# Feed-forward of a decoder layer: remainders at its start moved to VectorE, twelve loads in flight and results finished in place in its second product

## The chip, the cores and the metric

The kernel runs one layer of a decoder on one core of a Trainium2 chip. The metric is the device time of one execution in microseconds; the median of several runs is compared. The clock of the matrix engine (TensorE, "PE" in the profile) has two levels here, 2.4 GHz (granted clock 1.00) and 1.2 GHz (0.50).

## The reference, cut to what matters

The layer has two sub-layers. The change touches only the second, the feed-forward, and its tail:

```python
h = rms_norm(x, g_pre_ffn[l]) * (1.0 + scale_f) + shift_f       # x: (1, 1024, 1024) float32
gu = h @ w_ffn_in[l]                                             # 1024 x 5632
g_part, u_part = gu[..., :D_FF], gu[..., D_FF:]                  # D_FF = 2816 = 22 * 128
y = (jax.nn.silu(g_part) * u_part) @ w_ffn_out[l]                # 2816 x 1024
x = x + gate_f * rms_norm(y, g_post_ffn[l])
```

## The kernel before, in words

All products are float32. Each operand is split into a rounded part `hi` and a remainder `lo = value - hi`; `product` issues three matmuls for every product of blocks (hi*hi, hi*lo, lo*hi). ScalarE ("ACT") makes the `hi`, GpSimd ("POOL") or VectorE ("DVE") the `lo`, SyncE ("SP") issues the DMAs. Every engine runs its own instructions in the order written; semaphores tie them. There is no scheduler: the order in the code is the order on the engine.

**First product** (`h @ w_ffn_in`). Of the 22 column tiles of gate and up, two are computed plainly (`up`, four weight units `N_FF` to `N_FF+3`), 20 (`NW`) by a Winograd-like scheme of seven products of half-size blocks (`wino`, 84 matmuls a tile). It needs four sums of blocks of the activations, T1 to T4 (`t_part` on VectorE, 16 pieces), their `hi` (`t_hi_part`, ScalarE) and their `lo` (`t_lo_part`, GpSimd, L883); for each tile four weight sums (`s_part`, VectorE, L1719), seven `hi` (`ws_hi_part`, ScalarE, L1188) and seven `lo` (`ws_lo_part`, GpSimd, L888); and `ff_pair` (VectorE, L1747 to L1764) puts the seven results together, with two SiLUs on ScalarE. The remainders of the last two plain units are `split_plain` on GpSimd (L894). The stretch in which the plain tiles run, while T1 to T4 and the operands of the first Winograd tile are made, is called the turn.

**Sums for the second product.** `w_ffn_out` takes part in the same kind of scheme with eleven (`KF`) row pairs. For each of them `load_w2` brings 1 MB into `w2t`, GpSimd makes four differences (`add_w2`, L923) in `w2s`, and `store_w2` writes 1 MB to `w2sum_dram`. There is one `w2t` and one `w2s`, so set j+1 cannot be loaded before set j's sums are made, nor summed before set j is stored. GpSimd makes set 0 between the remainders of Winograd tiles 0 and 1, sets 1 to 9 inside its loop, set 10 after the loop. Before the last tile's results ScalarE waits for all 44 sums (`act.wait_ge(w2_sum, 4 * KF)`), and SP stores set 10 before it issues the first loads of the second product, since these use the same memory.

**Second product** (`... @ w_ffn_out`). 77 steps (`DN`): seven products P1, P5, P6, P3, P7, P2, P4 of eleven steps each, twelve matmuls a step (`down`). For step m `load_down` (L717) loads two or three tiles of 256 KB, `add_down` (VectorE, L1810) makes the left sum two steps ahead, `down_hi` (ScalarE, L1257, L1259) and `remainders` (VectorE, L1728, L1731) split both operands into one of eight slots (`RING`). A load may be issued when the load eight places earlier has been consumed. P1 has two loads a step, kept in `a_keep` and `b_keep`; P5 three (A21, A22, T1). `evac_down` adds finished products from PSUM.

**Tail.** For each of eight row tiles: multiply both halves with the column factor `grow` into `fin` (L1854, L1855; for tiles 4 to 7 the right half in `c22`, L1846), reciprocal root of the mean square (squares on ScalarE in `z_square`, L1276; L1857 to L1862), `fin * rstd + x1r` (L1865), and `store_tile`. `fin` has two slots, so from tile 2 on the multiplication waits until an earlier tile has been written out. PSUM of tiles 4 to 7 is complete one tile after another at the end of the last five steps.

Of the kernel before, what the change touches and what calls it, by code (L numbers as in the profile page):

```python
# [25 lines left out]
P = 128  # L26
# [13 lines left out]
def hybrid_layer(nc, x, c, positions, w_ada, b_ada, g_pre_mix, g_post_mix, w_in, b_f, sinks,  # L40
# [166 lines left out]
    RING = 8  # L207
# [8 lines left out]
    dn_raw = [at(f"dn_raw{r}", H0 + (32 * (r // 4) + 4 * (r % 4)) * KB, [P, NT]) for r in range(RING)]  # L216
# [7 lines left out]
    fin = at("fin", R0 + 80 * KB, [P, 2, D])  # L224
# [180 lines left out]

    def dn_src(m, what):
# [3 lines left out]
        return dn_raw[raw_no[m, what] % RING][:, :]  # L410

# [20 lines left out]
    for m in sorted(evacs):  # L432
        p, tt = evacs[m]
        if p >= 2:
            n_ev += {3: 2, 4: 2}.get(p, 1)
            ev_no[p, tt] = n_ev
    SQUARES = [(t, 1) for t in range(NTOK)] + [(t, 0) for t in range(NTOK)]
# [7 lines left out]
    with ExitStack() as ctx:  # L445
# [9 lines left out]
        tile_in = [sem(f"tile_in{k}") for k in range(KD)]  # L455
# [22 lines left out]
        dve_step, pool_step, act_step = sem("dve_step"), sem("pool_step"), sem("act_step")  # L478
# [7 lines left out]
        gcol_ok, diag_ok, grow_ready, grow_ok = sem("gcol_ok"), sem("diag_ok"), sem("grow_ready"), sem("grow_ok")  # L486
# [16 lines left out]
        done = [sem("done0"), sem("done1")]  # L503
# [16 lines left out]
        def _(sp):  # L520
# [159 lines left out]
            with sp.Fori(0, NW // 2 - 1) as it:  # L680
                store_w2(it)
                load_w2(it + 1)
                for par in range(2):
                    sp.wait_ge(fs_lo, it * (2 * NPR) + NPR * (par + 1))
                    load_raw(par, it * (2 * P) + (PLAIN + 2 + par) * P)
                    store_ff(it * 2 + (1 + par), 1 - par, it * 4 + (8 + 2 * par))

            def store_tile(t):
                for hb in range(2):
                    cols = slice(hb * NT, (hb + 1) * NT)  # L690
                    sp.wait_ge(fin_ok, 2 * t + hb + 1)
                    sp.dma_start(out_v[t][:, cols], fin[:, t % 2, cols]).then_inc(done[t % 2], 16)
# [9 lines left out]
            def load_down(m, what, ahead):  # L702
                name, j = dn_step_of(m)
                q = load_no[m, what]
                if q >= RING:
                    sp.wait_ge(*consumed(*ahead[q - RING]))
                row, col = int(what[1]) - 1, int(what[-1]) - 1
                if what[0] == "T":
                    sp.wait_ge(w2_out, 16 * (j + 1))
# [7 lines left out]
                sp.dma_start(dn_src(m, what), src).then_inc(tile_in[q % RING], 16)  # L717
# [7 lines left out]
            for m, what in order_of_loads[:RING]:  # L725
# [4 lines left out]
            sp.wait_ge(w2_out, 16 * KF)  # L730
            for m, what in order_of_loads[RING:]:
# [11 lines left out]
            for i in range(2):  # L743
                sp.wait_ge(done[i], 2 * 16 * (NTOK // 2))

        @block.gpsimd
        def _(pool):
# [132 lines left out]
            def t_lo_part(q):  # L880
                name, k = T_ORDER[q]
                pool.wait_ge(t_hi, q + 1)
                pool.tensor_tensor(t_hl[name][1][:, k], t_fp32(name, k)[:, :], t_hl[name][0][:, k].bitcast(F32), ALU.subtract)\  # L883
                    .then_inc(t_lo, 1)

# [5 lines left out]
            def split_plain(j):  # L891
                n = N_FF + 2 + j
                pool.wait_ge(w_hi_ok, n + 1)
                pool.tensor_tensor(w_hl[1][:, n % 2], wraw[:, n % 2], w_hl[0][:, n % 2].bitcast(F32), ALU.subtract)\  # L894
                    .then_inc(w_split, 1)

            for q in range(2):
                t_lo_part(q)
            split_plain(0)
            for q in range(2, 6):  # L900
                t_lo_part(q)
            split_plain(1)
            for q in range(6, 12):
                t_lo_part(q)
            for i in range(4):
                ws_lo_part(0, 0, i)
            for q in range(12, 16):
                t_lo_part(q)
            for i in range(4, NPR):
                ws_lo_part(0, 0, i)  # L910

            def add_w2(it, what, first):
                n = W2_SUMS.index(what)
# [3 lines left out]
                if what == "T1":  # L917
                    pool.wait_ge(w2t_in, it * 32 + 32)
                    if not first:
                        pool.wait_ge(w2_out, it * 16)  # L920
# [4 lines left out]
            pool.wait_ge(ff_ready, 8)  # L925
            for what in W2_SUMS:
                add_w2(0, what, True)
# [8 lines left out]
            for what in W2_SUMS:  # L936
                add_w2(KF - 1, what, False)

        @block.scalar
        def _(act):  # L940
# [303 lines left out]
            def loaded(m, what):  # L1244
                q = load_no[m, what]
                act.wait_ge(tile_in[q % RING], 32 + 16 * (q // RING + 1))
# [32 lines left out]
            for m in range(3, DN):  # L1279
# [5 lines left out]
                if DN - KF <= m < DN - KF + NTOK:  # L1285
                    z_square(m - DN + KF)
            for t in range(NTOK):
                z_square(NTOK + t)
                act.wait_ge(z_var, t + 1)
# [3 lines left out]
        def _(dve):  # L1293
# [9 lines left out]
            nc.vector.memset(credit[:, 1:2], 0.0).then_inc(ff_ok, 4)  # L1303

# [397 lines left out]

            def mult_plain(ff, ch):
# [17 lines left out]
            def loaded(m, what):  # L1721
                q = load_no[m, what]
                dve.wait_ge(tile_in[q % RING], 32 + 16 * (q // RING + 1))
# [42 lines left out]
            for q in range(8):  # L1766
                t_part(q)
            mult_plain(0, 0)
            for q in range(8, 12):
                t_part(q)  # L1770
            for k in range(KH, KD):
# [4 lines left out]
            for q in range(12, 16):  # L1776
                t_part(q)
            mult_plain(1, 0)
            mult_plain(1, 1)
# [574 lines left out]
```

## Time and profile before

| | us |
|---|---|
| median of 3 runs | 1503.3 (1502.32 to 1504.65) |
| profiled execution, its own time | 1501.47 |
| its span on the core | 1499.7 |
| TensorE busy | 1413.5 (94%) |
| VectorE, ScalarE, GpSimd busy | 977.8, 550.6, 614.3 |
| mean granted clock of TensorE | 0.988 |

Positions are microseconds from the start of the span. The first product with its turn reaches from about 816 to 1261, the second product from 1261 to 1484.5, the tail from there to the end. A matmul of 128x512 is shown with 0.39 us, but they are pipelined: two neighbours start 0.227 us apart at full clock. In a row of the timeline the bracket gives the idle time of the engine ahead of the instruction and what ended it.

### The profile page before, as it was taken

How to read it: one execution, taken by the hardware profiler on the slowest of the kernel's cores; microseconds unless marked ns; L12 is line 12 of the kernel's file. 1: busy time of each engine (PE TensorE's matmuls, PEld its weight loads, DVE VectorE, ACT ScalarE, POOL GpSimd, SP SyncE). 2: the span in 40 equal slices, each digit the busy share in tenths (PEclk: the TensorE clock that was granted, in tenths of full speed). 3: DMA queues.
4: the chain of work that ended last, by engine and by line, in shares of the span. 5: the costliest groups of instructions: out<-in, count | busy, mean ns of one | idle time of the engine just before them, and what ended most of it. 6: DMA issues, size and time to landing. Idle time of an engine off the chain costs nothing. (4 is left out here: it accounts for less than half of the span.)

```text
span 1499.7 us, 19843 instructions
## 1 busy us (share of the span) xinstructions
PE 1413.5 (94%) x6923; PEld 1153.7 (77%) x6923; DVE 977.8 (65%) x1410; ACT 550.6 (37%) x1122; POOL 614.3 (41%) x500
## 2 busy tenths in 40 slices
PE   4899898999999999999999899999999999899995
PEld 2898676777768888888878677888888887678884
DVE  4776867555554766666665877766666664578677
ACT  3711367554552000112243433333333333454452
POOL 0315735242345544334211888766666662000000
PEclk9999999999999999999999999999999999999998
DMA  9401111121222645432332136444444434656754
GB/s 349 130 15 29 48 39 40 53 63 43 92 57 92 165 130 145 121 113 85 99 113 99 52 106 193 140 140 140 140 140 140 140 112 161 225 180 213 245 169 168
DMA packets 174635, 184.63 MB, mean 123 GB/s; under 512 B 15872, under 2 KB 128600, under 8 KB 174048
## 3 DMA queue, kind: packets, MB, share of 16 engines
q1 hardware_dynamic: 168336, 178.87, 38.2%
q10 hardware_dynamic: 6224, 4.77, 1.0%
q8 instruction: 45, 0.74, 0.2%
q14 instruction: 30, 0.25, 0.1%
HBM read 147.94 MB, written 35.68 MB: 122 GB/s over the span
## 5 line engine op out<-in xcount | busy, mean ns | idle before, releaser
L1474 DVE TENSOR_TENSOR pt_lo<-PS,pt_hi 128x512 fp32r<-128x512 f32 (+3 forms) x128 | 74.5, 582 | 97.5 <-ACT pt_hi L1045 97.1
L888 POOL TENSOR_TENSOR ws_lo<-s_tmp,ws_hi 128x512 fp32r<-128x512 f32 x80 | 114.0, 1429 | 58.6 <-ACT ws_hi L1188 58.6
L1874 PE MATMUL PS<-db_hi,da_hi 128*128 128x512 f32 x308 | 121.7, 395 | 8.6 <-DVE db_lo L1731 8.5
L1874 PE MATMUL PS<-T_hi,ws_hi 128*128 128x512 f32 x320 | 124.6, 389 | 1.0 <-POOL ws_lo L888 1.0
L1874 PE MATMUL PS<-T_hi,ws_lo 128*128 128x512 f32 x320 | 124.5, 389 | 0.0
L1874 PE MATMUL PS<-T_lo,ws_hi 128*128 128x512 f32 x320 | 124.5, 389 | 0.0
L1874 PE MATMUL PS<-db_hi,da_lo 128*128 128x512 f32 x308 | 121.3, 394 | 0.0
L1874 PE MATMUL PS<-db_lo,da_hi 128*128 128x512 f32 x308 | 121.1, 393 | 0.0
L1874 PE MATMUL PS<-act_hi,w_hi 128*128 128x512 f32 x288 | 113.8, 395 | 3.1 <-POOL w_lo L894 3.1
L794 POOL CAST w_hi<-wraw 128x1024 fp32r<-128x1024 f32 x39 | 43.0, 1102 | 174.3 <-PE PS L1874 113.0
L1874 PE MATMUL PS<-act_lo,w_hi 128*128 128x512 f32 x288 | 112.7, 391 | 0.0
L1874 PE MATMUL PS<-act_hi,w_lo 128*128 128x512 f32 x288 | 112.6, 391 | 0.0
L1045 ACT ACTIVATE pt_hi<-PS 128x512 fp32r<-128x512 f32 (+3 forms) x128 | 65.2, 510 | 119.7 <-PE PS L2080 101.5
L2001 PE MATMUL PS<-act_hi,w_hi 128*128 128x512 f32 x240 | 95.7, 399 | 5.6 <-DVE nm L1455 5.1
L796 POOL TENSOR_TENSOR w_lo<-wraw,w_hi 128x1024 fp32r<-128x1024 f32 x39 | 99.6, 2553 | 3.2
L1874 PE MATMUL PS<-act_hi,ws_hi 128*128 128x512 f32 x240 | 94.3, 393 | 5.0 <-POOL ws_lo L888 5.0
L836 POOL TENSOR_SCALAR s_row<-s_row,rden 128x128 f32<-128x128 f32 (+7 forms) x64 | 47.1, 749 | 123.9 <-DVE rden L1469 123.8
L2001 PE MATMUL PS<-act_hi,w_lo 128*128 128x512 f32 x240 | 96.1, 400 | 0.0
L2001 PE MATMUL PS<-act_lo,w_hi 128*128 128x512 f32 x240 | 94.4, 393 | 0.0
L1874 PE MATMUL PS<-act_hi,ws_lo 128*128 128x512 f32 x240 | 94.1, 392 | 0.0
L1874 PE MATMUL PS<-act_lo,ws_hi 128*128 128x512 f32 x240 | 93.9, 391 | 0.0
L1106 ACT ACTIVATE sg<-PS 128x512 f32<-128x512 f32 x28 | 16.8, 599 | 207.6 <-PE PS L1874 207.6
(310 smaller groups left out, 3743.1 us busy)
## 6 DMA issues: line engine op xcount, KB each, us to landing
dn_raw<-ff_dram SPq DMA_DIRECT2D x66, 256.0 KB, 3.7
adaraw<-in_w_ada_dram SPq DMA_DIRECT2D x32, 512.0 KB, 4.1
wraw<-in_w_in_dram SPq DMA_DIRECT2D x25, 512.0 KB
wraw<-in_w_ffn_in_dram SPq DMA_DIRECT2D x24, 512.0 KB, 5.1
ff_dram<-sl SPq DMA_DIRECT2D x22, 512.0 KB, 6.6
w2t<-in_w_ffn_out_dram SPq DMA_DIRECT2D x22, 512.0 KB, 6.8
w2sum_dram<-w2s SPq DMA_DIRECT2D x11, 1024.0 KB, 5.8
dn_raw<-w2sum_dram SPq DMA_DIRECT2D x44, 256.0 KB, 3.9
```

The lines of the kernel that those rows point to most:

```text
L794: pool.tensor_copy(w_hl[0][:, slot], wraw[:, slot]).then_inc(w_hi_ok, 1)
L796: pool.tensor_tensor(w_hl[1][:, slot], wraw[:, slot], w_hl[0][:, slot].bitcast(F32), ALU.subtract)\
L836: ins = pool.tensor_scalar(pr, pr, rden[:, r % 4, hd:hd + 1], 1.0, ALU.mult, ALU.mult)
L888: pool.tensor_tensor(ws_hl[i][1][:, :, :], left(par, i), ws_hl[i][0][:, :, :].bitcast(F32), ALU.subtract)\
L1045: nc.scalar.activation(pt_hl[gp % 3][0][:, 0:n], PS[:, 4 + gp % 2, 0:n], ACT.Copy).then_inc(grp_hi, 1)
L1106: nc.scalar.activation(sg[:, j], PS[:, j], ACT.Sigmoid).then_inc(g_done, 1)
L1474: nc.vector.tensor_tensor(pt_hl[gp % 3][1][:, 0:n], PS[:, 4 + gp % 2, 0:n], pt_hl[gp % 3][0][:, 0:n].bitcast(F32), ALU.subtract).then_inc( ...
L1874: ins = nc.tensor.matmul(out_ap, lhs[a], rhs[b], start=first and i == 0, stop=last and i == 2)
L2001: ins = nc.tensor.matmul(PS[:, bank], w_hl[a][:, n % 2, k], act_hl[b][:, k, ch * NT:(ch + 1) * NT], start=(m == 0), stop=(m == 3 * KD - 1))
```

## The change

1. At the turn the 16 remainders of T1 to T4, the two of the plain units and the seven of Winograd tile 0 go from GpSimd to VectorE (`t_lo_part`, `unit_lo`, `first_lo`). GpSimd has no instruction left between the last `act_lo` and the remainders of tile 1.
2. The sums of `w_ffn_out` start in the loop: set `it` instead of set `it + 1` in iteration `it`, after i = 4 and 6 instead of 2 and 5. Sets 9 and 10 follow after the loop. SP stores a set and loads the next at the end of an iteration instead of at its start.
3. Loads of the second product: twelve slots (`LRING`) instead of eight, ten loads instead of eight ahead of the last two stores of the first product.
4. Squares and column factors of `c12`, `c22` and `c11` are made inside the steps of the second product; the roots of tiles 0 to 3 are made together; results are written in place (`c11`, `c12`, `usum`, `c22`), so no wait for an earlier store is left.

```diff
-    RING = 8
+    RING, LRING = 8, 12
...
+    SQUARE_AT = {KF * 5 - 1 + tt: tt for tt in range(4)}
+    GAIN_AT = {KF * 5 + 1 + tt: ("c12", tt) for tt in range(4)}
...
             with sp.Fori(0, NW // 2 - 1) as it:
-                store_w2(it)
-                load_w2(it + 1)
                 for par in range(2):
                     sp.wait_ge(fs_lo, it * (2 * NPR) + NPR * (par + 1))
                     load_raw(par, it * (2 * P) + (PLAIN + 2 + par) * P)
                     store_ff(it * 2 + (1 + par), 1 - par, it * 4 + (8 + 2 * par))
+                store_w2(it)
+                load_w2(it + 1)
...
-                if q >= RING:
-                    sp.wait_ge(*consumed(*ahead[q - RING]))
+                if q >= LRING:
+                    sp.wait_ge(*consumed(*ahead[q - LRING]))
...
-            for m, what in order_of_loads[:RING]:
+            for m, what in order_of_loads[:10]:
...
+            pool.wait_ge(fs_lo, NPR)
             with pool.Fori(0, NW // 2 - 1) as it:
                 for par in range(2):
                     for i in range(NPR):
                         ws_lo_part(it + par, 1 - par, i)
-                        if i in (2, 5):
-                            add_w2(it + 1, W2_SUMS[2 * par + (i == 5)], False)
+                        if i in (4, 6):
+                            add_w2(it, W2_SUMS[2 * par + (i == 6)])
             for i in range(NPR):
                 ws_lo_part(NW // 2 - 1, 1, i)
-            for what in W2_SUMS:
-                add_w2(KF - 1, what, False)
+            for j in (KF - 2, KF - 1):
+                for what in W2_SUMS:
+                    add_w2(j, what)
...
+            def z_rstd(t0, t1, nth):
+                cols, sq = slice(24 + t0, 24 + t1), ssq_z[:, 2 * t0:2 * t1].rearrange("p (t h) -> p t h", h=2)
...
+            def finish(t, halves, sources):
+                dve.wait_ge(x1r_in[t % 2], 32 if t < 4 else 64)
...
+            gain("c11", 3)
+            z_rstd(0, 4, 1)
+            for t in range(4):
+                finish(t, (c11[t], c12[t]), (c11[t][:, :], c12[t][:, :]))
```

On VectorE at the turn, where T3 is finished and the first plain column tile is multiplied, there stood before (`h_old`, `h_new` hold the activations and then T1 to T4):

```order
L1701 TENSOR_TENSOR h_new_182<-h_new_186,h_new_182 128x512
L1701 TENSOR_TENSOR h_new_183<-h_new_187,h_new_183 128x512
L1701 TENSOR_TENSOR h_new_184<-h_new_188,h_new_184 128x512
L1706 TENSOR_TENSOR sl<-PS,sl 128x512
L1701 TENSOR_TENSOR h_new_185<-h_new_185,h_old_189 128x512
```

and now, on the same engine at the same place:

```order
L1682 TENSOR_TENSOR h_new_184<-h_new_188,h_new_184 128x512
L1687 TENSOR_TENSOR T_lo<-h_old_189,T_hi 128x512
L1687 TENSOR_TENSOR T_lo<-h_old_190,T_hi 128x512
L1687 TENSOR_TENSOR T_lo<-h_old_191,T_hi 128x512
L1687 TENSOR_TENSOR T_lo<-h_old_192,T_hi 128x512
L1704 TENSOR_TENSOR sl<-PS,sl 128x512
L1693 TENSOR_TENSOR w_lo<-wraw,w_hi 128x1024
L1682 TENSOR_TENSOR h_new_185<-h_new_185,h_old_189 128x512
```

Four remainders of T1 and the remainder of the third plain unit came in.

On GpSimd at the end of the first product, its last instructions before (with the semaphores each waits for):

```order
L888 TENSOR_TENSOR ws_lo_217<-wraw,ws_hi_216 128x512 [waits fs_hi]
L888 TENSOR_TENSOR ws_lo_219<-wraw,ws_hi_218 128x512 [waits fs_hi]
L923 TENSOR_TENSOR w2s<-w2t 128x512 [waits w2_out,w2t_in]
L923 TENSOR_TENSOR w2s<-w2t 128x512
L923 TENSOR_TENSOR w2s<-w2t,w2s 128x512 [waits w2_sum] x2
```

and its last instructions now:

```order
L890 TENSOR_TENSOR ws_lo_217<-wraw,ws_hi_216 128x512 [waits fs_hi]
L890 TENSOR_TENSOR ws_lo_219<-wraw,ws_hi_218 128x512 [waits fs_hi]
L902 TENSOR_TENSOR w2s<-w2t 128x512 [waits w2_out,w2t_in]
L902 TENSOR_TENSOR w2s<-w2t 128x512
L902 TENSOR_TENSOR w2s<-w2t,w2s 128x512 [waits w2_sum] x2
L902 TENSOR_TENSOR w2s<-w2t 128x512 [waits w2_out,w2t_in]
L902 TENSOR_TENSOR w2s<-w2t 128x512
L902 TENSOR_TENSOR w2s<-w2t,w2s 128x512 [waits w2_sum] x2
```

A second set of four came in, and its first instruction waits for the store of the set before it and for its own load.

## Rows read from the trace of the kernel before

**Rows 1.** The head of the page: the span.

```profile
span 1499.7 us, 19843 instructions
```

**Rows 2.** Waits of TensorE: waiting line, releaser, us in total, times, longest.

```profile
PE PS L1874 <- DVE db_lo L1731: 8.5, 6, 1.8
...
PE PS L1874 <- POOL ws_lo L888: 6.0, 3, 3.0
...
PE PS L1874 <- POOL w_lo L894: 3.1, 1, 3.1
```

**Rows 3.** Timeline of TensorE: start, duration, instruction, idle time ahead of it.

```profile
848.30 0.77 PE L1874 MATMUL PS<-act_hi,w_hi 128*128 128x512 f32 x1 [3.14 <-POOL w_lo L894]
848.86 0.63 PE L1874 MATMUL PS<-act_lo,w_hi 128*128 128x512 f32 x1
849.29 0.63 PE L1874 MATMUL PS<-act_hi,w_lo 128*128 128x512 f32 x1
...
1261.04 0.39 PE L1874 MATMUL PS<-db_hi,da_hi 128*128 128x512 f32 x1
...
1484.10 0.39 PE L1874 MATMUL PS<-db_hi,da_lo 128*128 128x512 f32 x1
```

**Rows 4.** Chain that ended last, from step 19 of the second product: start, length.

```profile
1326.42 136.32 PE PS L1874 x600
```

**Rows 5.** Timeline of VectorE and of GpSimd at the turn.

```profile
827.72 10.37 POOL L877 TENSOR_TENSOR act_lo<-h_new,act_hi 128x512 fp32r<-128x512 f32 x8 [33.19 <-DVE h_new L1662]
...
835.81 6.23 DVE L1701 TENSOR_TENSOR h_old<-h_new,h_old 128x512 f32<-128x512 f32 x4
841.96 2.48 DVE L1701 TENSOR_TENSOR h_new<-h_new,h_new 128x512 f32<-128x512 f32 x4
...
845.64 2.51 POOL L894 TENSOR_TENSOR w_lo<-wraw,w_hi 128x1024 fp32r<-128x1024 f32 x1 [4.15 <-ACT w_hi L1215]
```

**Rows 6.** Timeline of GpSimd, ScalarE and VectorE at the first product's end.

```profile
1247.11 2.64 POOL L923 TENSOR_TENSOR w2s<-w2t,w2s 128x512 f32<-128x512 f32 x2
...
1250.11 0.60 ACT L1193 ACTIVATE p1c<-PS 128x512 f32<-128x512 f32 x1 [7.28 <-POOL w2s L923]
...
1255.66 0.63 ACT L1257 ACTIVATE da_hi<-a_keep 128x512 fp32r<-128x512 f32 x1 [4.46 <-DMA a_keep<-ff_dram]
...
1258.40 0.69 DVE L1750 TENSOR_TENSOR sl<-PS,u_sum 128x512 f32<-128x512 f32 x1
...
1262.53 0.68 DVE L1731 TENSOR_TENSOR db_lo<-b_keep,db_hi 128x512 fp32r<-128x512 f32 x1
```

**Rows 7.** A set of sums in the loop (timelines of SP, GpSimd); landing of `w2t`.

```profile
924.87 0.62 SPq L676 DMA_DIRECT2D w2sum_dram<-w2s  x1
...
933.89 1.60 POOL L923 TENSOR_TENSOR w2s<-w2t 128x512 f32<-128x512 f32 x1 [2.85 <-DMA w2t<-in_w_ffn_out_dram]
...
DMA to landing us min/median/max: 3.6/6.8/8.3
```

**Rows 8.** P5: a step on VectorE; VectorE's waits; DMA traffic 1269 to 1281.

```profile
1310.08 0.69 DVE L1810 TENSOR_TENSOR s_keep<-dn_raw,dn_raw 128x512 f32<-128x512 f32 x1 [2.96 <-DMA dn_raw<-ff_dram]
...
DVE s_keep L1810 <- DMA dn_raw<-ff_dram: 26.1, 9, 3.1
...
DMA packets 2308, 4.21 MB, mean 351 GB/s; under 512 B 252, under 2 KB 252, under 8 KB 2308
```

**Rows 9.** Timeline of VectorE in the tail.

```profile
1464.64 0.69 DVE L1854 TENSOR_TENSOR fin<-c,grow 128x512 f32<-128x512 f32 x1
...
1479.46 2.87 DVE L1846 TENSOR_TENSOR c<-c,grow 128x512 f32<-128x512 f32 x4
1482.37 0.69 DVE L1851 TENSOR_TENSOR usum<-PS,usum 128x512 f32<-128x512 f32 x1
...
1486.07 0.68 DVE L1851 TENSOR_TENSOR usum<-PS,usum 128x512 f32<-128x512 f32 x1
...
1496.48 0.75 DVE L1865 SCALAR_TENSOR_TENSOR fin<-c,rstd,x1r 128x512 f32<-128x512 f32 x1
```

More of the change, by code:

```diff
@@ L404, in hybrid_layer, with landed @@
             sum_no[m] = len(sum_no) + 1
+    def landed(q):
+        return (32 if q % LRING < KD else 0) + 16 * (q // LRING + 1)
     def dn_src(m, what):
@@ L436, in hybrid_layer @@
             ev_no[p, tt] = n_ev
+    SQUARE_AT = {KF * 5 - 1 + tt: tt for tt in range(4)}
+    SQUARE_AT.update({KF * 5 + 9 + tt: 4 + tt for tt in range(4)})
+    SQUARE_AT.update({evac_step(5, tt) + 1: NTOK + tt for tt in range(4)})
+    GAIN_AT = {KF * 5 + 1 + tt: ("c12", tt) for tt in range(4)}
+    GAIN_AT.update({KF * 6 + 1 + tt: ("c22", tt) for tt in range(4)})
+    GAIN_AT.update({min(evac_step(5, tt) + 2, DN - 1): ("c11", tt) for tt in range(3)})
     SQUARES = [(t, 1) for t in range(NTOK)] + [(t, 0) for t in range(NTOK)]
@@ L454, in hybrid_layer @@
         ada2_in = [sem("ada2_in0"), sem("ada2_in1")]
-        tile_in = [sem(f"tile_in{k}") for k in range(KD)]
+        tile_in = [sem(f"tile_in{k}") for k in range(LRING)]
         w_in_s = [sem("w_in_s0"), sem("w_in_s1")]
@@ L742, in _ @@
                 store_tile(t)
-            for i in range(2):
-                sp.wait_ge(done[i], 2 * 16 * (NTOK // 2))
+            sp.wait_ge(done, 2 * 16 * NTOK)
         @block.gpsimd
@@ L889, in ws_lo_part, with add_w2 @@
                     .then_inc(fs_lo, 1)
[L891 to L913, printed above, removed]
+            def add_w2(it, what):
                 b11, b12, b21, b22 = [w2t[:, i, c * NT:(c + 1) * NT] for i in range(2) for c in range(2)]
@@ L918, in add_w2 @@
                     pool.wait_ge(w2t_in, it * 32 + 32)
-                    if not first:
-                        pool.wait_ge(w2_out, it * 16)
+                    pool.wait_ge(w2_out, it * 16 + 16)
                 elif what != "T3":
@@ L1767, in _ @@
                 t_part(q)
+            for q in range(4):
+                t_lo_part(q)
             mult_plain(0, 0)
+            unit_lo(0)
             for q in range(8, 12):
                 t_part(q)
+            for q in range(4, 8):
+                t_lo_part(q)
+            unit_lo(1)
+            for q in range(8, 12):
+                t_lo_part(q)
             for k in range(KH, KD):
@@ L1777, in _ @@
                 t_part(q)
+            for i in range(4):
+                first_lo(i)
+            for q in range(12, 16):
+                t_lo_part(q)
             mult_plain(1, 0)
             mult_plain(1, 1)
+            for i in range(4, NPR):
+                first_lo(i)
             with dve.Fori(0, NW // 2 - 1) as it:
@@ L1866, in _ @@
+            def finish(t, halves, sources):
+                dve.wait_ge(x1r_in[t % 2], 32 if t < 4 else 64)
+                for hb in range(2):
+                    nc.vector.scalar_tensor_tensor(out=halves[hb][:, :], in0=sources[hb], scalar=rstd[:, 24 + t:25 + t],
                                                    in1=x1r[:, t % 4, hb * NT:(hb + 1) * NT], op0=ALU.mult, op1=ALU.add)\
                         .then_inc(fin_ok, 1)
+            gain("c11", 3)
+            z_rstd(0, 4, 1)
+            for t in range(4):
+                finish(t, (c11[t], c12[t]), (c11[t][:, :], c12[t][:, :]))
@@ new lines, in _ @@
+            for t in range(4, NTOK):
+                tt = t - 4
+                dve.wait_ge(z_ready, tt + 1)
+                nc.vector.tensor_tensor(usum[tt][:, :], PS[:, dn_bank(NPR - 1, tt)], usum[tt][:, :], ALU.add).then_inc(dn_ev, 1)
+                dve.wait_ge(dn_ev, n_ev + tt + 1)
+                link(nc.vector.tensor_tensor(fin[:, t % 2], usum[tt][:, :], grow[:, 1, 0:NT], ALU.mult))
+                z_rstd(t, t + 1, t - 2)
+                finish(t, (usum[tt], c22[tt]), (fin[:, t % 2], c22[tt][:, :]))
```

101 lines of the change are left out of this document (47 added, 54 removed).

## The prediction, made before the change was timed

> **What bounds the kernel now.** I read the waits of TensorE first, then its timeline, then the timelines of those it waits for. TensorE is busy 94% of the span, so time can only be won where it pauses, where its clock is low, and behind its last matmul. The waits of the stretches that the change touches are three short lists: 3.1 us for the remainder of a plain unit, 6.0 us in three pauses for GpSimd's weight remainders, 8.5 us in six pauses for VectorE's remainders in the second product [rows 2]. What they cost in all comes from counting. At full clock 600 matmuls fill 136.32 us, 0.227 us each [rows 4]. From 848.30 to 1261.04, 412.7 us, stand 1776 matmuls, worth 402.6: **10.1 us lost**. It is the 6.0 of pauses, 17 matmuls at half clock (0.43 us apart instead of 0.227, as at 848.86 and 849.29), 3.4 us, and 0.7 of restarting [rows 2, 3]. From 1261.04 to 1484.10 stand 923 intervals, worth 209.3 of 223.1: **13.8 us lost**: 8.5 of pauses, the rest clock and restarts. Behind TensorE's end (1484.5) the tail takes **15.2 us** to 1499.7 [rows 1, 3].
>
> **The turn.** 25 instructions leave GpSimd, two of them of double width: 27 units of 128x512. VectorE needs 1.56 us a unit while GpSimd works beside it and 0.62 when it does not (the fours at 835.81 and 841.96) [rows 5]. GpSimd's last `act_lo` ends at 838.1 and it now stands idle from there to the end of tile 0's remainders, so I take 0.62. The T1 sums speed up after 838 and end at about 839.5 instead of 842; T3's four end at 841.9; four T remainders at 844.4, the multiplication at 845.0, the unit's remainder (two units, 1.24) at 846.3; ScalarE's `hi` for it, ready at 845.6 before, moves ahead with the T1 sums. TensorE resumes at 846.4 instead of 848.3 [rows 3, 5]: −1.9 us. From there VectorE has about 27 units, 16.8 us, until tile 0's first remainder is there at about 863.5, and TensorE wants it 96 matmuls (21.8 us) after 846.4, at 868.2. A slack of 4.7 us. The pause behind set 0 of the sums and that behind the load of set 1 vanish with these sums, and SP is no longer held by them ahead of the next raw weights. In the loop GpSimd has 19 us a tile (84 matmuls) for nine instructions of 1.3 to 1.6 us [rows 6, 7], so I cost the new places of the sums at nothing; the cover is a whole tile between a remainder and its use. The turn: −1.9 −10.1 = **−12.0** (bounds −12.3 and −9.5: 1.8 us of the 10.1 are the low clock behind a pause of 3.1 us, which a pause of 1.4 us may keep, and a small rest may stay).
>
> What the row shows of the two engines side by side, 1.56 against 0.62 us, has a rule. The Trainium skill (SBUF — State Buffer, section Who interferes with whom) says that a VectorE instruction with two SBUF inputs and a GpSimd instruction that reads SBUF exclude each other on a shared port. By this rule the 27 units cost 0.62 each with GpSimd idle, the sum above; without it, at 1.56, they would be 25 us later, which is the slower rival below.
>
> **End of the first product.** Here the change adds something that its words do not mention. Before, GpSimd makes only set 10 after the last tile's remainders, ended at 1249.75; then SP stores it and issues the first loads of the second product, and ScalarE, which waits for all sums, copies the last tile's first result at 1250.11 after 7.28 us [rows 6]. The remaining chain is fixed: load landed and `hi` at 1255.66, VectorE's remainders, two additions, the second at 1258.40 to 1259.09, which frees TensorE for step 0 at 1259.2 [rows 6]. TensorE comes at 1261.04, so the slack is **1.8 us** [rows 3]. Now set 9 is made in that place, until the same 1249.75. Only then does SP store it and load set 10, and GpSimd waits for both. In the loop store to next sum took 9.0 us (924.87 to 933.89) with 1 MB of raw weights behind it; the load itself lands after 3.6 to 8.3, median 6.8 [rows 7]. Without raw weights I take 8.5 (bounds 5.5 and 10). Then four sums at 1.3 (1247.11: two in 2.64): 5.2 [rows 6]. The sums end 13.7 us later, at 1263.5. SP and ScalarE are both held until then. Step 0 can start at 1263.5 + 9.45 = 1273.0. Step 1 needs the remainder that began at 1262.53, 12.8 us behind the sums, ended 0.6 later, so it starts at 1277.0 and not 2.72 us after step 0: 1.3 more [rows 6]. The stall is 13.7 − 1.8 + 1.3 = **+13.2** (bounds +9.9 and +16). So long a pause will bring a low clock behind it; nearest are the 9 slow matmuls behind the 3.1 us [rows 3]: **+1.9** (bounds 0 and +3.5).
>
> By the Trainium skill (DMA: Bandwidth & Descriptors, section Anatomy of one DMA) a transfer takes 2.0 us and its bytes over 436 GB/s. By that page, store and load, 2.1 MB, would take 6.8 us instead of my 8.5 and the forecast would be 1.7 us lower; the trace has 351 GB/s in its densest stretch [rows 8].
>
> **Second product.** In P5 the load of A22 waits for a remainder that VectorE makes immediately before it wants that A22. So every step shows the full landing, 2.9 us (26.1 in 9), plus three instructions, 1.9: 4.8 us, where TensorE needs 2.72 [rows 4, 8]. With twelve places the load waits for a step that lies two VectorE steps further back: two steps must cover 1.2 us of issuing and one landing of 3 to 4 us, 2.1 to 2.6 us a step. Traffic: 0.79 MB a step at 351 GB/s is 2.2 us [rows 8]. Both are below 2.72, and P1 gives a start of some steps. I count all 13.8 us of loss as gone except 0.1: **−13.7** (bounds −13.9 and −9; P5 may still lose some if landings lengthen with twelve loads under way). The pause at step 4, two loads too few ahead of the last store, goes too: ten cover steps 0 to 4, and step 5 is loaded as soon after that store as step 4 was.
>
> **Tail.** Before, VectorE makes tiles 0 to 3 from 1464.64, then the four factors of `c22` (2.87 us), and reaches tile 4 at 1482.37 though its PSUM was complete at 1474.3, three groups of 15 matmuls ahead of the end; the tiles follow 3.70 us apart (1482.37, 1486.07), the last instruction starts at 1496.48 [rows 9]. Now twelve multiplications lie in steps in which VectorE has 2.72 us for two to four instructions of 0.6, the roots of four tiles are one, and tiles 0 to 3 need eight instructions of 0.72: from 1464.7 about 8.2 us, to 1473. Tile 4 starts at 1474.3, tile 7 at 1474.3 + 3 x 3.70 = 1485.4 instead of 1493.5: −8.1. The waits for `x1r` of tiles 4 and 6 together may take 0.6. **−7.5** (bounds −8.5 and −5.5).
>
> **Sum** against the profiled execution: 1501.47 − 12.0 + 13.2 + 1.9 − 13.7 − 7.5 = 1483.4. The median of the runs lies 1.8 above that execution; the same on top gives 1503.3 − 18.1 = **1485.2**. Bounds all one way: 1478.4 and 1498.8.
>
> **Rivals.**
> *No stall at the transition.* If ScalarE and SP were not held by set 10, or its load were early, 15.1 us less: 1470.1. For it: the step's purpose would be met. Against: the order on GpSimd, the single `w2t`, and the 7.28 us that ScalarE already waits. 10%.
> *The twelve slots do not help.* P5 keeps 4.8 us a step because landings lengthen: +11.8 us, 1497.0. Against: DMA had 3 loads per 4.8 us to move there, far from 351 GB/s. 6%.
> *Slower: VectorE is late in the turn.* It decides at 0.80 us a unit: (868.2 − 846.4)/27. At the 1.56 of 835.81, GpSimd or not, tile 0 would begin 27 x 0.94 − 4.7 = 20.7 us late, and the first plain unit some 5 more; instead of −12.0 the turn gives about +17: 1485.2 + 29 = 1514. For it: GpSimd's turn to help is over exactly where VectorE has most to do. Against: 2.48 us for four with GpSimd idle [rows 5]. 4%.
>
> **How the numbers follow.** My forecast has 80%, these three 20%. The range leaves out the first rival, the slower one and thin edges of the forecast, 2 in 10: 1476 to 1496. A measurement of this kernel can tell about 0.2%, 3 us. Faster 0.94, same 0.02, slower 0.04: the slower rival holds all that is slower, and the forecast's upper bound, 1498.8, is still faster.
>
> **What will show it.** TensorE resumes its third plain unit at about 846.4 and then has no pause up to its last Winograd tile. Before the second product it waits 12 us, released by VectorE's `db_lo` or `sl`; ScalarE's `p1c` of the last tile shows 20 us of waiting for the sums. GpSimd shows a wait of some 8 us for `w2t` ahead of set 10. No pause over 0.5 us in P5. From TensorE's end to the span's end 7.7 us. I am wrong if GpSimd's set 10 begins at once, if P5 still pauses, or if VectorE's T remainders take over 0.8 us.

## The result, and the profile after

| | before | after |
|---|---|---|
| median of 4 runs each, us | 1503.97 (1502.32 to 1505.50) | 1486.44 (1483.91 to 1487.61) |
| profiled execution, us | 1501.47 | 1486.08 |
| its span, us | 1499.7 | 1484.4 |

The changed kernel takes 0.9881 of the time before, 95% interval 0.9864 to 0.9899: 17.5 us less. The forecast was 1485.2 us, range 1476 to 1496.

The page of the changed kernel, its head, and the waits of TensorE from 820 us on (engine, what it works on, what released it, then total us, times, longest), to be held against [rows 1, 2]:

```profile
span 1484.4 us, 19819 instructions
...
PE 1406.5 (95%) x6915; PEld 1152.1 (78%) x6923; DVE 981.1 (66%) x1427; ACT 550.4 (37%) x1119; POOL 586.0 (39%) x475
```

```profile
PE PS L1891 <- DVE sl L1748: 12.3, 1, 12.3
...
PE PS L1891 <- DVE w_lo L1693: 1.4, 1, 1.4
```

The ten pauses of [rows 2] have become two: 1.4 us at the turn, and one of 12.3 us. (Five pauses of 0.4 to 0.7 us ahead of the turn, released by `h_new`, stand in both kernels and are left out.) The timeline of TensorE shows where they lie (start, duration, line, idle time ahead in the bracket):

```profile
846.42 0.47 PE L1891 MATMUL PS<-act_hi,w_hi 128*128 128x512 f32 x1 [1.40 <-DVE w_lo L1693]
...
1248.85 0.39 PE L1891 MATMUL PS<-T_hi,ws_lo 128*128 128x512 f32 x1
1261.56 0.77 PE L1891 MATMUL PS<-db_hi,da_hi 128*128 128x512 f32 x1 [12.32 <-DVE sl L1748]
1262.12 0.63 PE L1891 MATMUL PS<-db_lo,da_hi 128*128 128x512 f32 x1
1262.55 0.63 PE L1891 MATMUL PS<-db_hi,da_lo 128*128 128x512 f32 x1
```

The last Winograd matmul starts at 1248.85 (before 1260.81), and the 12 us won up to there are waited away ahead of the second product. Its first matmuls then run 0.43 us apart, at the half clock. The chain that made TensorE wait, from the timelines of GpSimd, SyncE, ScalarE:

```profile
1232.19 2.99 POOL L902 TENSOR_TENSOR w2s<-w2t 128x512 f32<-128x512 f32 x2
...
1237.81 0.55 SPq L686 DMA_DIRECT2D w2sum_dram<-w2s  x1
1238.40 1.69 SPq L682 DMA_DIRECT2D w2t<-in_w_ffn_out_dram  x2
...
1246.68 2.53 POOL L902 TENSOR_TENSOR w2s<-w2t 128x512 f32<-128x512 f32 x2 [8.90 <-DMA w2t<-in_w_ffn_out_dram]
1249.17 2.60 POOL L902 TENSOR_TENSOR w2s<-w2t,w2s 128x512 f32<-128x512 f32 x2
...
1252.13 0.60 ACT L1171 ACTIVATE p1c<-PS 128x512 f32<-128x512 f32 x1 [21.27 <-POOL w2s L902]
```

GpSimd makes set 9 from 1232.19, SP stores it and loads set 10, GpSimd waits 8.90 us for it, and its sums end at 1251.77. ScalarE stands idle for 21.27 us ahead of the copy of the last tile's first result. Only then do `sl` and the first step of the second product follow (TensorE's bracket above).

From there TensorE has no further pause; the chain of work that ended last holds the second product as one link, then the tail:

```profile
1261.56 182.69 PE PS L1891 x792
...
1461.66 7.66 DMA x1r<-x_dram
1469.41 0.75 DVE usum L1869
```

The tail on VectorE (compare [rows 9]):

```profile
1463.98 0.69 DVE L1880 TENSOR_TENSOR usum<-PS,usum 128x512 f32<-128x512 f32 x1 [2.16 <-PE PS L1891]
...
1469.41 0.75 DVE L1869 SCALAR_TENSOR_TENSOR usum<-fin,rstd,x1r 128x512 f32<-128x512 f32 x1 [3.09 <-DMA x1r<-x_dram]
...
1470.74 0.69 DVE L1880 TENSOR_TENSOR usum<-PS,usum 128x512 f32<-128x512 f32 x1
...
1478.13 0.68 DVE L1880 TENSOR_TENSOR usum<-PS,usum 128x512 f32<-128x512 f32 x1
...
1481.15 0.75 DVE L1869 SCALAR_TENSOR_TENSOR c<-c,rstd,x1r 128x512 f32<-128x512 f32 x1
```

VectorE is idle when tile 4's PSUM is complete (1463.98), but `fin * rstd + x1r` then waits 3.09 us for `x1r`. TensorE's last matmul starts at 1473.76 and ends at 1474.15; 10.2 us follow. The load that lands last here is tile 6's (issued at 1461.66, landed after 7.66 us). Tile 4's own was issued at 1458.26 and landed after 4.2 us, 3.8 us before the instruction could use it (its issue, and the landing of this one load):

```profile
1458.26 0.46 SPq L749 DMA_DIRECT2D x1r<-x_dram  x1
...
DMA to landing us min/median/max: 4.2/4.2/4.2
```

The 15.3 us between the two spans, by marks that both timelines have:

| stretch | before | after | difference | forecast |
|---|---|---|---|---|
| start to last Winograd matmul | 1260.81 | 1248.85 | −12.0 | −12.0 |
| from there to step 0 of the second product | 0.23 | 12.71 | +12.5 | +13.2 |
| step 0 to the last matmul | 223.06 | 212.20 | −10.9 | −11.8 (−13.7 +1.9) |
| end of TensorE to end of span | 15.2 | 10.2 | −5.0 | −7.5 |
| sum | 1499.7 | 1484.4 | −15.3 | −18.1 |

Three of the four stretches came within 1 us of the forecast. Whether for the reasons given is what the experiments ask.

### The profile page after: what moved, and what is told of

Its sections match the earlier page's. It is cut to its first block and busy times, and to the rows that moved or that the text cites. A ratio compares the mean times of both kernels' runs of the same rounds, so it can differ in the third digit from the quotient of the medians.

```text
span 1484.4 us, 19819 instructions
## 1 busy us (share of the span) xinstructions
PE 1406.5 (95%) x6915; PEld 1152.1 (78%) x6923; DVE 981.1 (66%) x1427; ACT 550.4 (37%) x1119; POOL 586.0 (39%) x475
## 5 line engine op out<-in xcount | busy, mean ns | idle before, releaser
L1891 PE MATMUL PS<-db_hi,da_hi 128*128 128x512 f32 x308 | 121.2, 393 | 12.3 <-DVE sl L1748 12.3
```

The source lines that it names most:

```text
L1891: ins = nc.tensor.matmul(out_ap, lhs[a], rhs[b], start=first and i == 0, stop=last and i == 2)
```

## Experiments

All start from the changed kernel, so they are compared with 1486.44. Each was timed beside the kernel before on its chip, whose medians there were 1502.4 to 1503.7; differences of medians below some 2 us mean little, and where a difference is that small the positions within one profile decide. "Length of the turn" below is from the last matmul ahead of the third plain unit to the last Winograd matmul: 416.0 us before (844.77 to 1260.81), 404.2 after (844.64 to 1248.85).

**1. The sums at the turn again.** Part 2 undone, but with the places (4, 6) in the loop.

```diff
 # SP
             with sp.Fori(0, NW // 2 - 1) as it:
+                store_w2(it)
+                load_w2(it + 1)
                 for par in range(2):
...
-                store_w2(it)
-                load_w2(it + 1)
 # GpSimd
             pool.wait_ge(fs_lo, NPR)
+            for what in W2_SUMS:
+                add_w2(0, what)
...
-                            add_w2(it, W2_SUMS[2 * par + (i == 6)])
+                            add_w2(it + 1, W2_SUMS[2 * par + (i == 6)])
...
-            for j in (KF - 2, KF - 1):
-                for what in W2_SUMS:
-                    add_w2(j, what)
+            for what in W2_SUMS:
+                add_w2(KF - 1, what)
```

> The changed kernel with one part undone: GpSimd makes a set of column sums again before the loop over the Winograd tiles (behind the last plain unit, at the turn), the loop makes the set of the next pair, and only set 10 is left behind it. Theory (the late sums are the whole cause of TensorE's 12.3 us wait ahead of the second product, and that wait is the cause of the half-clock matmuls after it): set 10 ends near 1237.5 us instead of 1251.8, before the last Winograd matmul (1248.9), TensorE's wait on sl before its first step falls from 12.3 us to under 1 us, the 15 matmuls at 0.43 us go, 12.5 + 2.9 = 15.4 us less, of which up to 2 us come back as a shorter pause on a later step: 1471 to 1473 us. The turn stays as it is, since GpSimd is idle from 838 to 872 us and its sums there start only behind the last first-tile remainder (877 us). Rival 1: what holds the first step is VectorE's and ScalarE's own work of the last tile, so that a pause of 4 us or more stays: 1476 to 1480 us. Rival 2: the sums at the turn make the remainders of the second Winograd tile late and TensorE pauses near 890 us for 3 us or more: 1475 to 1478 us.

Measured: 1472.34 us (1470.65 to 1473.58), 0.9805 of before (0.9789 to 0.9821), 14.1 us below the changed kernel. TensorE's waits and the last rows of GpSimd:

```profile
...
PE PS L1892 <- DVE w_lo L1694: 1.4, 1, 1.4
```

```profile
873.77 2.67 POOL L902 TENSOR_TENSOR w2s<-w2t 128x512 f32<-128x512 f32 x2 [35.44 <-issue]
876.39 2.65 POOL L902 TENSOR_TENSOR w2s<-w2t,w2s 128x512 f32<-128x512 f32 x2
...
1232.53 2.99 POOL L902 TENSOR_TENSOR w2s<-w2t 128x512 f32<-128x512 f32 x2
1235.48 2.64 POOL L902 TENSOR_TENSOR w2s<-w2t,w2s 128x512 f32<-128x512 f32 x2
```

Set 0 now stands at the end of the 35 us in which GpSimd is idle; set 10 ends at 1238.1, ahead of the last Winograd matmul (1249.19). The wait of 12.3 us is gone, and so is every matmul at half clock behind it (none from 836 us on); the length of the turn stays 404.2. Both rivals fall: nothing else holds the first step, and the sums at the turn cost nothing. So the whole stall was the late set: moving the sums into the loop, the main piece of part 2, made the kernel slower by 14 us.

**2. The remainders of the turn on GpSimd again.** Part 1 undone alone.

```diff
 # GpSimd, ahead of the loop: t_lo_part, split_plain and ws_lo_part(0, 0, i) in the order of before
+            for q in range(2):
+                t_lo_part(q)
+            split_plain(0)
...
 # VectorE
             for q in range(8):
                 t_part(q)
-            for q in range(4):
-                t_lo_part(q)
             mult_plain(0, 0)
-            unit_lo(0)
...
```

> The changed kernel with one part undone: the remainders of the T tiles, of the two plain units and of the first Winograd tile are on GpSimd again, in the order of the kernel before; the late sums, the twelve loads and the finishing in place stay. Theory: the two pauses, the wait before the third unit and the half clock behind them come back as they were, 12.0 us: 1486.4 + 12.0 = 1498.4 us (1496.5 to 1500), and the last Winograd matmul is issued near 1260.8 us instead of 1248.9. Rival: a part of the gain came from taking the first set of sums out of GpSimd's queue at the turn (it stood there from 886.6 to 893.0 us), not from VectorE: then fewer pauses return and the time is 1492 to 1496 us.

Measured: 1490.57 us (1489.79 to 1491.26), 4.1 above the changed kernel and not 12. The theory missed, and the time lies below the rival's 1492 to 1496 too, though the rival's mechanism is what the rows show. The waits of TensorE from 820 us on:

```profile
PE PS L1904 <- DVE sl L1775: 11.9, 1, 11.9
PE PS L1904 <- POOL w_lo L902: 3.2, 1, 3.2
...
PE PS L1904 <- POOL ws_lo L896: 1.1, 1, 1.1
```

Of the four pauses before, two come back, the unit's (3.2) and tile 0's (1.1); the two near 894 and 906 us do not. The length of the turn is 408.9. Before it was 416.0 and in the changed kernel 404.2, so 7.1 us of the 11.8 do not need VectorE, as long as set 0 is out of GpSimd's queue.

**3. Both undone.** The edits of experiments 1 and 2 in one kernel.

> The changed kernel with two parts undone together: the remainders at the turn are on GpSimd again, and the first set of column sums stands at the turn again (the edits of e1_sums_early and e2_turn_back in one). Theory from e2_turn_back: the four pauses of the kernel before at the turn had two causes. The two later ones (894.3 and 905.7 us, 5.3 us with the clock at full speed) need both, GpSimd's remainders and the set of sums in its queue from 886.6 to 893.0 us; each of the two edits alone removes them. So here they return, and the turn costs 12.0 us over e1_sums_early: 1472.3 + 12.0 = 1484.3 us (1483 to 1486). Rival: the two effects add up, and the sums at the turn cost nothing of their own: 1472.3 + 4.1 (e2_turn_back over the changed kernel) = 1476.4 us.

Measured: 1479.99 us (1479.19 to 1481.97), 7.6 above experiment 1: between the theory's 1484.3 and the rival's 1476.4, so neither held. The length of the turn is 413.0. The pause near 894 is back, the one near 906 is not:

```profile
PE PS L1905 <- POOL ws_lo L896: 3.3, 2, 2.2
PE PS L1905 <- POOL w_lo L902: 3.1, 1, 3.1
```

```profile
887.95 2.99 POOL L929 TENSOR_TENSOR w2s<-w2t 128x512 f32<-128x512 f32 x2
890.91 3.42 POOL L929 TENSOR_TENSOR w2s<-w2t,w2s 128x512 f32<-128x512 f32 x2
894.30 1.27 POOL L896 TENSOR_TENSOR ws_lo<-wraw,ws_hi 128x512 fp32r<-128x512 f32 x1
```

Set 0 stands 6.3 us ahead of tile 1's first remainder, and TensorE restarts behind that one at 895.6. Four medians now make a square:

| | set 0 at the turn | late sums |
|---|---|---|
| remainders on VectorE | 1472.34 | 1486.44 |
| remainders on GpSimd | 1479.99 | 1490.57 |

The effects do not add: moving the remainders to VectorE is worth 7.6 us with the set at the turn, 4.1 without it. In both rows the late sums lose more than they bring (14.1 and 10.6).

**4 and 5. The places of the sums in the loop.** Experiments 3 and 1, each with the places of the kernel before.

```diff
-                        if i in (4, 6):
-                            add_w2(it + 1, W2_SUMS[2 * par + (i == 6)])
+                        if i in (2, 5):
+                            add_w2(it + 1, W2_SUMS[2 * par + (i == 5)])
```

> e5_turn_sums with a third thing put back: inside the loop GpSimd makes the sums behind the third and sixth remainder of a tile, as in the kernel before, not behind the fifth and seventh. Theory: the fourth pause of the kernel before at the turn (2.95 us at 905.7 us, and the clock behind it) came from this place alone: the first sum of set 1 waits for its load (5.98 us in GpSimd's queue in the kernel before, at 903.2 us) and four remainders stand behind it. So the pause returns: 1480.0 + 12.0 - 7.65 = 1484.3 us (1483 to 1485.5). Rival: it came from the later start of everything at the turn, and the place does not matter: 1480 us.

Measured: 1481.73 us (1481.06 to 1483.71), 1.7 above experiment 3, where the theory had 4.3 and the rival 0; the turn is 414.7 long against 413.0 there. The pause near 906 is back, in the same place and for the reason given:

```profile
PE PS L1905 <- POOL ws_lo L896: 4.6, 3, 2.2
```

```profile
903.41 1.28 POOL L929 TENSOR_TENSOR w2s<-w2t 128x512 f32<-128x512 f32 x1 [6.04 <-DMA w2t<-in_w_ffn_out_dram]
904.65 2.51 POOL L896 TENSOR_TENSOR ws_lo<-s_tmp,ws_hi 128x512 fp32r<-128x512 f32 x2
```

It restarts TensorE at 905.97, where the kernel before did at 905.71, but it is 1.39 us long and not 2.95. The price was missed. In this execution the half clock fell behind the pause at 894 (matmuls 0.43 apart up to 899), TensorE reached the place 1.8 us later and waited 1.6 less; in the kernel before, the slow matmuls stood behind the last pause and came on top of it, and its turn is 416.0 long. So in these two executions the place where the clock fell decided whether the next pause hid the loss.

> e1_sums_early with the sums of the loop behind the third and sixth remainder, as in the kernel before; the remainders at the turn stay on VectorE. Theory: with VectorE making the first tile's remainders GpSimd is some 9 us ahead at the turn, the same wait for the load of set 1 falls at 884 to 889 us and the remainder behind it is wanted by TensorE no earlier than 896 us: no pause, 1472.3 us (1471 to 1474). Rival: the place costs a pause here too, 1475 us or more, and the gain at the turn then owes more to the place than to VectorE.

Measured: 1470.87 us (1470.41 to 1472.20), length of the turn 404.2, no pause. GpSimd waits for the load here as well, only 15.6 us earlier:

```profile
880.18 3.00 POOL L890 TENSOR_TENSOR ws_lo<-s_tmp,ws_hi 128x512 fp32r<-128x512 f32 x2
887.83 1.30 POOL L902 TENSOR_TENSOR w2s<-w2t 128x512 f32<-128x512 f32 x1 [4.65 <-DMA w2t<-in_w_ffn_out_dram]
```

So with the remainders on VectorE the place does not matter. Part 1 alone is worth the whole turn; the two others, set 0 out of the turn and the later places in the loop, each remove a piece of the same thing.

**6 and 7. How many loads under way.** Eight and nine places in the changed kernel.

```diff
-    RING, LRING = 8, 12
+    RING, LRING = 8, 8        # second kernel: 8, 9
...
-            for m, what in order_of_loads[:10]:
+            for m, what in order_of_loads[:8]:        # second kernel: [:9]
```

> The changed kernel with eight loads under way in the second product instead of twelve (the eight oldest places; eight are issued ahead instead of ten). Column factors stay in the steps, finishing stays in place. Theory: the number of places is what took away the pauses of 0.4 to 1.4 us in the fifth part of the second product; they come back, 9 to 13.9 us, and TensorE's chain in the second product is about 196 us long instead of 182.7: 1495.4 to 1500.3 us, most likely 1500. Rival: the pauses belonged to what stood in the queues with the loads and not to their number, so that eight places do as well: 1486 to 1488 us.

Measured: 1500.05 us (1498.82 to 1504.22), 13.6 above the changed kernel. The pauses are back, five of them in P5 and one of 0.55 us at step 4, the first whose loads are no longer issued ahead. VectorE shows the landing in every step, 4.7 to 4.9 us apart, as in [rows 8]:

```profile
PE PS L1891 <- DVE db_lo L1729: 8.9, 6, 1.9
```

```profile
1304.22 0.69 DVE L1822 TENSOR_TENSOR s_keep<-dn_raw,dn_raw 128x512 f32<-128x512 f32 x1 [2.97 <-DMA dn_raw<-ff_dram]
...
1308.92 0.69 DVE L1822 TENSOR_TENSOR s_keep<-dn_raw,dn_raw 128x512 f32<-128x512 f32 x1 [2.80 <-DMA dn_raw<-ff_dram]
...
1313.82 0.69 DVE L1822 TENSOR_TENSOR s_keep<-dn_raw,dn_raw 128x512 f32<-128x512 f32 x1 [3.00 <-DMA dn_raw<-ff_dram]
```

> The changed kernel with nine loads under way. Theory (a dependency, not a number of bytes in flight): with eight, the load of A22 waits for a remainder that VectorE makes one step ahead of the sum that wants it, 2.9 us of landing and 1.9 us of VectorE work a step, 4.8 us. With nine the load that waits is T1 of the step before, one VectorE step further back: two steps must cover two issues of 0.6, the landing of 2.9 and 1.9 of work, 6.0 us, 3.0 us a step against the 2.72 that TensorE needs, so some 0.3 us a step is left over nine steps: 1486.4 + 2.5 = 1489 us (1486.5 to 1491). Rival: the pauses fall in proportion to the places (13.6 us for four, 3.4 us each), as they would if bandwidth or the number of loads in flight set the pace: 1496.6 us.

Measured: 1489.46 us (1488.88 to 1490.27), 3.0 above. One place more recovers 10.6 of 13.6 us, which a pace set by traffic or by the number of loads would not give. The rows of VectorE and TensorE's wait, and between the first two steps the remainder that frees a place and the load that SP issues into it:

```profile
PE PS L1891 <- DVE db_lo L1729: 1.6, 3, 0.6
```

```profile
1308.90 0.68 DVE L1729 TENSOR_TENSOR db_lo<-dn_raw,db_hi 128x512 fp32r<-128x512 f32 x1
1309.61 0.33 SPq L726 DMA_DIRECT2D dn_raw<-w2sum_dram  x1
```

```profile
1311.32 0.69 DVE L1822 TENSOR_TENSOR s_keep<-dn_raw,dn_raw 128x512 f32<-128x512 f32 x1 [1.73 <-DMA dn_raw<-ff_dram]
...
1314.70 0.69 DVE L1822 TENSOR_TENSOR s_keep<-dn_raw,dn_raw 128x512 f32<-128x512 f32 x1 [1.49 <-DMA dn_raw<-ff_dram]
...
1318.30 0.69 DVE L1822 TENSOR_TENSOR s_keep<-dn_raw,dn_raw 128x512 f32<-128x512 f32 x1 [1.70 <-DMA dn_raw<-ff_dram]
```

The remainder ends at 1309.58 and the load of T1 is issued at 1309.61, with A21 and A22 of the next step right behind it; the sum that wants this A22 starts at 1314.70. This is the dependency of the theory. The total came as expected, the rate did not: a step takes 3.5 us there and not 3.0. The term that was off is the landing: the loads from `ff_dram` take 4.1 us here (2.9 with eight places), and 0.9 of issuing, 4.1 of landing and 1.9 of work are 6.9 us for two steps, near the 7.0 measured. TensorE still pauses only three times, for 1.6 us in all, where nine steps at 0.8 over its 2.72 would be 7 us. That the lead from P1 covers the rest is argued, not measured; so the total was right in part by luck. What sets the pace is which consumer frees the place that a load waits for.

**8. A semaphore for each place of `x1r`.**

```diff
-                sp.dma_start(x1r[:, t], x1_dram[t + 4]).then_inc(x1r_in[t % 2], 16)
+                sp.dma_start(x1r[:, t], x1_dram[t + 4]).then_inc(x1r_own[t % 4], 16)
...
-                dve.wait_ge(x1r_in[t % 2], 32 if t < 4 else 64)
+                dve.wait_ge(x1r_own[t % 4], (64 if t % 4 > 1 else 0) + (16 if t < 4 else 32))
```

> The changed kernel with a semaphore for each of the four places of x1r, so that tile 4 waits for its own load alone (as it stands tiles 4 and 6 wait for both their loads, and tiles 5 and 7 for both theirs). Nothing else changes. Theory: tile 4's load was issued at 1458.3 us and lands within 8 us, before 1466.3, when its factor is ready; the wait of 3.09 us at tile 4 goes, the three tiles behind it follow at 3.70 us as before, and the stretch from TensorE's end to the end of the span is 7.1 us instead of 10.2: 1483.4 us (1482.8 to 1484.0). Rival: the load of tile 4 itself lands late, because stores of 256 KB run beside it (landings up to 9.1 us): half of the wait or more stays, 1485 us or more.

Measured: 1484.15 us (1482.10 to 1484.94), 2.3 below the changed kernel; alone that would be within its scatter. Its VectorE rows at tile 4 decide:

```profile
1465.90 0.69 DVE L1881 TENSOR_TENSOR usum<-PS,usum 128x512 f32<-128x512 f32 x1 [2.16 <-PE PS L1892]
...
1468.27 0.75 DVE L1870 SCALAR_TENSOR_TENSOR usum<-fin,rstd,x1r 128x512 f32<-128x512 f32 x1
...
1469.60 0.68 DVE L1881 TENSOR_TENSOR usum<-PS,usum 128x512 f32<-128x512 f32 x1
```

From tile 4's sum to tile 5's are 3.70 us, as between the others, where the changed kernel had 6.76 (1463.98 to 1470.74). No wait for `x1r` is left, and from TensorE's end (1476.06) to the end of the span (1483.2) are 7.1 us. So the wait came from tile 6's load. But that the two share a semaphore is only half of the reason. The kernel before has the same semaphore and waits for a count of 48 at tile 4, which its own load completes:

```diff
-                dve.wait_ge(x1r_in[t % 2], 32 if t < 4 else 16 * (t // 2 + 1))    # before
+                dve.wait_ge(x1r_in[t % 2], 32 if t < 4 else 64)                   # changed
```

The change raised the count of tile 4 to 64, which needs tile 6's load as well. The count of 48 together with finishing in place was not run, so whether it is safe and as fast with both loads under way is not shown; a semaphore for each place avoids the question.

**9. The old tail.** Part 4 undone: squares, factors, `fin` with two slots and the waits for stores as in the kernel before.

```diff
-                if m in SQUARE_AT:
-                    z_square(SQUARE_AT[m])
+                if DN - KF <= m < DN - KF + NTOK:
+                    z_square(m - DN + KF)
...
+                if t >= 2:
+                    dve.wait_ge(done[t % 2], done_at[t % 2] + 2 * 16 * (t // 2))
...
```

> The changed kernel with the old finishing: column factors and squares where they stood in the kernel before, results made in fin with its two slots, stores waited for. Turn, late sums and twelve loads stay. Theory: the stretch from TensorE's end to the end of the span is 15.2 us again instead of 10.2, nothing else moves: 1486.4 + 5.0 = 1491.4 us (1490.5 to 1492.5). Rival: the factors and squares inside the steps cost TensorE nothing here but part of the loads' places changes the loads of the last part, so that the difference is under 3 us or over 7 us.

Measured: 1493.41 us (1492.52 to 1494.87), 7.0 above the changed kernel where 5.0 were expected, and outside the range. This kernel also has the old counts for `x1r`. In its profile TensorE's last matmul starts at 1477.61 and the span ends at 1493.1: 15.1 us behind its end, 4.9 more than 10.2, as expected. Turn and second product are as long as in the changed kernel (404.3 and 212.0). The rest lies ahead of the turn, where the two programs are the same: in the profiled execution, 1.5 us longer than the median, the matmul ahead of the third unit starts at 848.27 instead of 844.64, 3.6 us later. It is the clock: the granted clock was 0.88 from 40 to 80 us (0.93 in the changed kernel) and 0.96 from 240 to 280 (1.00), which is some 2.0 and 1.6 us of work at full clock. So I read part 4 as 5 us; why the clock was lower there stays open. The reason for the old length is seen where tile 4 begins:

```profile
1472.82 2.87 DVE L1863 TENSOR_TENSOR c<-c,grow 128x512 f32<-128x512 f32 x4
1475.72 0.69 DVE L1868 TENSOR_TENSOR usum<-PS,usum 128x512 f32<-128x512 f32 x1
```

**10. What the others point to.** Set 0 at the turn (experiment 1) and a semaphore for each place of `x1r` (experiment 8), with everything else as in the changed kernel.

> The changed kernel with the first set of column sums at the turn again (as e1_sums_early) and a semaphore for each place of x1r (as e4_x1r_own). Theory: the two do not touch each other. TensorE has no wait over 1 us in the second product, and the wait on x1r of 2.75 us at tile 4 goes: 1472.3 - 2.8 = 1469.5 us (1468.3 to 1470.8). Rival: without the wait another one stands at tile 4 (its own load lands late among the stores), 1471 us or more.

Measured: 1470.55 us (1468.13 to 1471.29, 5 runs), 0.9772 of before (0.9758 to 0.9786). It beats the kernel before by 33 us and the changed one by 16. Against experiment 1 the median is 1.8 lower, which the runs alone would not prove; in its profile the wait for `x1r` is gone and 7.2 us follow TensorE's end. Its remaining waits are those of experiment 1.

## Why the prediction was right or wrong

**The time** was right to 1.2 us, 1486.4 against 1485.2, and this is in part luck. Against the profiled executions the sum was 2.7 us too hopeful: the tail 2.5 and the second product with its clock 0.9 too much gain, the transition 0.7 too much loss. The forecast then put the median 1.8 us above the profiled execution, where it lies 0.4 above; this scatter hid about half of the miss.

The full-clock times of the prediction, 402.6 and 209.3 us, go by 0.2267 us a matmul and not by the 136.32/600 = 0.2272 of the row beside them. The runs bear out 0.2267: in experiment 1 the 923 intervals of the second product take 209.24 us.

**The turn, −12.0.** The size is exact. Third unit at 846.42 (forecast 846.4), no pause afterwards up to the last Winograd matmul, VectorE's T remainders in fours of 2.49 us. The reason was given half. I said that the pauses behind set 0 and behind the load of set 1 "vanish with these sums". They do (experiment 2), but they vanish as well when the sums stay and VectorE makes the remainders (experiments 1 and 5). With the sums gone, GpSimd can keep its remainders at a cost of 4.7 us; with the remainders on VectorE, the sums can stay at no cost. I had not asked what part 1 gives without part 2, and so did not see that part 2 had nothing left to win here. The slow pace of VectorE on which the slower rival rested did not return: VectorE took 0.62 us a unit with GpSimd idle beside it, which agrees with the rule of the Trainium skill that I cited (SBUF — State Buffer, section Who interferes with whom). No run here made GpSimd busy beside VectorE's 27 units, so the point from which that rival decides was not tested.

**The transition, +13.2.** The mechanism was as told in all links but one: set 9 where set 10 was, store, load, 8.90 us of waiting (forecast 8.5), sums 14.0 us later (13.7), ScalarE held 21 us, TensorE 12.3. Experiment 1 is the proof. The 1.3 us for step 1 did not come. Its remainder is late, but TensorE ran step 0 at half clock and came later itself, so nothing was to be waited for. The term was 12.5. The two DMAs in it, the store of set 9 and the load of set 10, took 8.9 us from the store's issue to the sum behind the load; the prediction had 8.5 from rows and 6.8 by the Trainium skill (DMA: Bandwidth & Descriptors, section Anatomy of one DMA), whose fit is for transfers that GpSimd issues, while SyncE issues these.

**The clock, +1.9.** Mis-sized: 923 intervals took 212.20 us where 209.3 are full clock, 2.9 us. The slow matmuls behind a pause of 3.1 us were the wrong measure for one of 12.3: the prediction counted 9 there, of which 6 stand the full 0.43 us apart in the trace; behind 12.3 us it was 13.

**The second product, −13.7.** Right: no pause is left, and experiments 6 and 7 confirm that it is the consumer on which the load waits. Eight places cost 13.6 us. One size was off: with twelve loads under way the loads from `ff_dram` landed after 5.8 us and not 3 to 4. VectorE waited for them, but TensorE never did.

**The tail, −7.5.** This is the step that failed: −5.0. I gave the waits for `x1r` of tiles 4 and 6 together 0.6 us; tile 4 alone waited 3.09. Two things came together. The change raised the count that tile 4 waits for from 48 to 64, so that it waits for tile 6's load too, and the prediction did not price this. And that load landed late, 7.66 us after its issue at 1461.66 between stores of 256 KB. Finishing in place makes eight results in 5.4 us, so that stores and loads come in one bunch: the four loads of `x1r` in the tail have a median of 6.7 us, against 4.7 in the kernel before and 4.7 in experiment 9, where the old finishing spreads them out. Experiment 8 removes the wait: 7.1 us behind TensorE's end, where the prediction had 7.7 with 0.6 of waiting in it.

**The rivals.** No stall at the transition: false as a forecast, but its 1470.1 is what experiment 1 gave once the late set was removed (1472.3; the missing 2 us are the tail). Twelve slots without use: false. VectorE late: false.

## What to carry to other kernels

When an engine is relieved of work in one place, ask first whether the pauses there are then gone already, before moving its other work away as well: here the second move bought nothing and put a load and a sum at the one place where all engines wait. Where a ring of buffers throttles, look at which consumer frees the place that the stalled load needs; one more place can be worth most of what four are. When two transfers share a semaphore, look at the count that each consumer waits for: a count that needs both makes it wait for the later one, and faster finishing bunches the stores just where that load must land.

## What the runs showed of the hardware

- Behind TensorE's pause of 12.3 us its granted clock was 0.89 over 1261 to 1291 us, with 13 matmuls 0.43 us apart. Behind 3.1 us at the turn (before) 6 stood so, from 848.86 to 851.42; behind the 1.4 us at the turn none, in any of the seven profiles with that pause.
- The half clock fell behind the pause at 894 us in one program (experiment 4) and behind that at 906 in another with nearly the same pauses up to there (before); both restart near 906 (905.97 and 905.71).
- In experiment 8 the granted clock was 0.83 from 830 to 850 us, where the changed kernel, with the same code there, shows 1.00. Executions of one kernel differed by 3 us and more, and with them the mean clock (the changed kernel: 0.991 at 1483.91 us, 0.988 at 1487.61).
- In the tail of the changed kernel a load of 512 KB among stores of 256 KB landed after 7.66 us, where the median of the four in the tail before was 4.7. From 1450 us on the twelve stores out of `c`, most of them in that bunch, have a median of 3.3 us, the four out of `usum`, each issued 3 us or more behind the store ahead of it, 2.0.
- From 1304 to 1316 us, in P5, the loads of 256 KB from `ff_dram` landed after a median of 2.9 us with eight places, 4.1 with nine and 5.8 with twelve.
